# Overflow blocks of a mixture of experts: two places for their inputs and sums, products of neighbouring blocks interleaved, and the row gathers moved by one block

## The chip, the core and the metric

The kernel runs on 1 core of one Trainium2 chip. The metric is device time in microseconds (us) of one execution. The engines are TensorE (PE), VectorE (DVE), ScalarE (ACT), GpSimd (POOL) and SyncE (SP, which here only issues transfers). Each engine works through its own list of instructions in order, and they meet through semaphores.

## The reference, cut to what matters

A layer with a convolution, a sparse attention and a mixture of 64 experts (8 per token, 512 tokens, width 1024, hidden width 256) is followed by two more layers. The change lies in the mixture of experts:

```
D_MODEL = 1024
SEQ = 512
N_EXPERTS = 64
TOP_K_EXPERTS = 8
EXPERT_DIM = 256
DISPATCH_BLOCK = 128
...
def swiglu(x, w1, w3, w2):
    return (jax.nn.silu(x @ w1) * (x @ w3)) @ w2
...
    def expert_block(args):
        e, toks, gs = args
        xb = t[toks]
        return swiglu(xb, w1[e], w3[e], w2[e]) * gs[:, None]

    out = lax.map(expert_block, (block_e, row_tok.reshape(n_blk, DISPATCH_BLOCK),
                                 row_g.reshape(n_blk, DISPATCH_BLOCK)))
    routed = jax.ops.segment_sum(out.reshape(rows, D), row_tok, num_segments=n_tok)
```

## The kernel before, in words

**Experts.** A step n = 0 to 63 computes one expert for up to 128 of its tokens. POOL gathers their rows from `h2rows` into XG (an indirect transfer). PE turns them (`pe_xt`), ACT and DVE make a high and a low part (XTh, XTl), and PE forms three products for each pair of parts, six matmuls per chunk of weights ("a product" below is such a group of six). Four chunks give gate and up (PS bank 0 or 1), then come Silu on ACT (SG), the gated hidden row HG on DVE, two small transposes on PE, HHh on ACT and HHl on DVE, and two chunks of the down product into PS banks 6 and 7. ACT copies those to YS, and POOL adds YS to `expert_sum` in memory with an indirect transfer (the scatter, L2127). The weights come in through `eraw`; ACT splits off a high part (wh) and DVE the rest (wl) in a ring of four places.

**Overflow blocks.** Where an expert has more than 128 tokens, the rest is computed after the 64 experts in blocks of at most 128 rows. A table TB, made on the chip, holds their count at TB[2] and for block p its expert and a code for its row list. Each engine reads the count and enters block p by a branch (`more_blocks`, L2359). With these inputs there are 3 blocks (p = 0, 1, 2). The code is written per engine in `block_(p, i)`; i is 0 here. The gathers of blocks 0 and 1 are issued in steps 60 and 61, on POOL, by `more_gather` (L2140).

In block p POOL does, in this order: `more_gate(p + 1)` (copies the gate column of block p + 1, then `drain`), the copy YIXC of block p's list, `more_gather(p + 2)` (copies the list IDXC, `drain`, issues the gather), waits for YS, scatters (L2433), waits for the gather p + 2 and for its own scatter, and only then goes on with block p + 1. It gathers for blocks 3 and 4 as well, though there are none: PE turns the rows of block p + 1 in block p always, and the counts of the semaphores rest on it. After the last block POOL raises `rows_whole`, on which SP waits to load the sums from memory (YF, L2396), and PE for what follows.

PE does in block p: four up products, the transposes of block p + 1's rows (L2163), the transposes of HG (L2457), two down products. Inputs, sums and gated rows of the blocks have one place each (XTh[:, 0], PS[:, 0], HG[:, 0]). DVE and ACT split the weights of block p + 1's first two chunks behind block p's HHl and XTh.

## Time and profile before

| | |
|---|---|
| median of 3 runs | 2372.37 us (2371.32 to 2376.65) |
| the profiled execution's own time | 2377.54 us |
| its span | 2375.7 us |
| PE busy in the span | 2256.5 us (95%) |
| POOL busy in the span | 286.1 us (12%) |
| the overflow blocks, from their first product on PE to `rows_whole` | 1060.9 to 1108.0 us |

The span is the part of the execution that the profiler sees from the first to the last instruction; all places in the trace below are us from its start. The page says "PE 77%" for the chain that ended last, so most of the program is bound by PE; the stretch from 1052 to 1108 us is read apart, since the change touches nothing else.

### The profile page before, as it was taken

Reading aid. Unit: us, or ns where it says so; the run is one execution under the profiler, and the core shown is the slowest. Engines: PE = TensorE matmul, PEld = TensorE weight load, DVE = VectorE, ACT = ScalarE, POOL = GpSimd, SP = SyncE. Lnnn points to the kernel's source line nnn. Section 1 sums busy time; section 2 is a strip of 40 time slices with the busy share of each in tenths; the row PEclk is TensorE's granted clock in tenths of the full one; section 3 lists DMA queues with packets and bytes.
Section 4 is the critical chain, followed back from the end, with each engine's and each line's share of the span. In section 5 each row is a group of like instructions: output and inputs, shape, how many; then the busy total and the mean of one; then the engine's idle time right before and its main releaser. Section 6 shows DMA issues by size and latency. Waiting matters only on the chain.

```text
span 2375.7 us, 30540 instructions
## 1 busy us (share of the span) xinstructions
PE 2256.5 (95%) x10226; PEld 1760.5 (74%) x10226; DVE 1536.6 (65%) x2363; ACT 1198.8 (50%) x1774; POOL 286.1 (12%) x248
## 2 busy tenths in 40 slices
PE   7999999899999999985999999999999789999997
PEld 5776666778888888874766788888788557888885
DVE  7788766899999999985564643333452766433344
ACT  4432444588888888874334332333222763323333
POOL 0000000344334433431000000000020000000000
PEclk9998999999999999998999999999999999999999
DMA  8511245799999999995210132223222001322332
GB/s 330 176 59 58 80 169 172 266 354 397 388 393 387 391 392 393 391 334 156 80 63 18 62 107 96 97 97 107 89 98 98 19 27 61 116 98 92 102 106 80
DMA packets 107615, 415.70 MB, mean 175 GB/s; under 512 B 20305, under 2 KB 32849, under 8 KB 82784
## 3 DMA queue, kind: packets, MB, share of 16 engines
q1 hardware_dynamic: 87408, 378.47, 42.5%
q0 software_dynamic: 19648, 34.73, 5.9%
q8 instruction: 71, 1.16, 0.2%
q10 hardware_dynamic: 432, 0.87, 0.1%
q14 instruction: 56, 0.46, 0.1%
HBM read 409.23 MB, written 43.65 MB: 191 GB/s over the span
## 4 chain that ended last, share of the span: by engine, by line
PE 77%; DVE 9%; issue 5%; ACT 4%; DMA 2%; DVEq 2%; POOLq 0%; SPq 0%; POOL 0%; ACTq 0%
PE PS L298 22%; PE PS L300 21%; PE PS L299 21%; PE PS L714 3%; DVE wl L197 2%; PE PS L2007 2%; ACT wh L192 2%; PE PS L736 2%; PE PS L725 1%; DMA ada_wa<-wada 1%; DMA expert_sum<-YS,YIXC 1%; PE PS L2032 1%; DVE XTl L2060 1%; PE PS L1245 1%; DVEq L1285 1%
## 5 line engine op out<-in xcount | busy, mean ns | idle before, releaser
L197 DVE TENSOR_TENSOR wl<-raw,wh 128x1024 fp32r<-128x1024 f32 x239 | 292.5, 1225 | 357.2 <-ACT wh L192 351.0
L298 PE MATMUL PS<-HTh,wh 128*128 128x512 f32 x1248 | 499.9, 401 | 6.0 <-ACT V L881 2.2
L299 PE MATMUL PS<-HTl,wh 128*128 128x512 f32 x1248 | 487.8, 391 | 0.0
L300 PE MATMUL PS<-HTh,wl 128*128 128x512 f32 x1248 | 487.6, 391 | 0.0
L197 DVE TENSOR_TENSOR wl<-eraw,wh 128x1024 fp32r<-128x1024 f32 x384 | 457.7, 1219 | 16.6 <-ACT wh L192 13.6
L192 ACT ACTIVATE wh<-raw 128x1024 fp32r<-128x1024 f32 x239 | 252.0, 1056 | 369.9 <-PE PS L300 346.1
L192 ACT ACTIVATE wh<-eraw 128x1024 fp32r<-128x1024 f32 x384 | 392.6, 1054 | 17.0 <-PE PS L300 14.7
L298 PEld LDWEIGHTS PS<-HTh,wh 128*128 128x128 f32 x1248 | 235.3, 189 | 72.2 <-issue 13.6
L299 PEld LDWEIGHTS PS<-HTl,wh 128*128 128x128 f32 x1248 | 235.5, 189 | 50.2 <-issue 3.4
L300 PEld LDWEIGHTS PS<-HTh,wl 128*128 128x128 f32 x1248 | 235.3, 189 | 49.8
L298 PE MATMUL PS<-wh,XTh 128*128 128x512 f32 x536 | 221.1, 412 | 4.0 <-DVE wl L2192 2.8
L300 PE MATMUL PS<-wh,XTl 128*128 128x512 f32 x536 | 210.4, 392 | 0.0
L299 PE MATMUL PS<-wl,XTh 128*128 128x512 f32 x536 | 209.3, 390 | 0.0
L2127 POOL DMA_INDIRECT expert_sum<-YS,IDX x64 | 115.0, 1796 | 343.2 <-ACT YS L2091 211.3
L298 PE MATMUL PS<-AFh,wh 128*128 128x512 f32 x352 | 138.5, 394 | 0.0
L300 PE MATMUL PS<-AFh,wl 128*128 128x512 f32 x352 | 137.0, 389 | 0.0
L299 PE MATMUL PS<-AFl,wh 128*128 128x512 f32 x352 | 137.0, 389 | 0.0
L947 ACT ACTIVATE AFh<-AFf 128x512 f32 (+1 forms) x44 | 27.8, 632 | 182.4 <-DVEq L957 182.4
L298 PEld LDWEIGHTS PS<-wh,XTh 128*128 128x128 f32 x536 | 100.8, 188 | 23.4 <-DVE wl L2192 4.0
L300 PEld LDWEIGHTS PS<-wh,XTl 128*128 128x128 f32 x536 | 100.6, 188 | 22.2
L299 PEld LDWEIGHTS PS<-wl,XTh 128*128 128x128 f32 x536 | 101.2, 189 | 16.9
L298 PE MATMUL PS<-wh,HHh 128*128 128x512 f32 x268 | 105.6, 394 | 4.5 <-DVE HHl L2509 2.8
(412 smaller groups left out, 3439.7 us busy)
## 6 DMA issues: line engine op xcount, KB each, us to landing
eraw<-wstream SPq DMA_DIRECT2D x192, 1024.0 KB, 9.9
raw<-wstream SPq DMA_DIRECT2D x240, 512.0 KB, 3.3
ada_w<-wada SPq DMA_DIRECT2D x20, 512.0 KB, 5.9
eraw<-wexp SPq DMA_DIRECT2D x9, 1024.0 KB, 6.6
ada_wb<-wada SPq DMA_DIRECT2D x2, 2048.0 KB, 15.5
ada_l<-wada SPq DMA_DIRECT2D x8, 512.0 KB, 3.4
ada_g<-wada SPq DMA_DIRECT2D x2, 2048.0 KB, 10.3
expert_sum<-LM SPq DMA_DIRECT2D x8, 512.0 KB, 6.4
```

Source lines behind the costliest of these rows:

```text
L192: nc.scalar.activation(wh[:, ci % RING, :], src, ACT.Copy).then_inc(split_high, 1)
L197: nc.vector.tensor_tensor(wl[:, ci % RING, :], src, wh[:, ci % RING, :].bitcast(F32), ALU.subtract).then_inc(split_done, 1)
L298: nc.tensor.matmul(o, lh, rh, start=start, stop=False)
L299: nc.tensor.matmul(o, lh, rl, start=False, stop=False)
L300: return nc.tensor.matmul(o, ll, rh, start=False, stop=stop)
L714: mm = nc.tensor.matmul(PS[:, sbank(u, m), 0:P * (j + 1)], q[:, j * P:(j + 1) * P], k[:, 0:P * (j + 1)], start=x == 0, stop=x == len(prods ...
L725: mm = nc.tensor.transpose(PS[:, 4 + u % 2, kb * P:(kb + 1) * P], E_[:, u % 3, 0, kb * P:(kb + 1) * P], const("ident"))
L736: mm = nc.tensor.matmul(o, values(h, kb), Pt[:, u % 2, kb * P:(kb + 1) * P], start=kb == 0, stop=kb == j)
L947: nc.scalar.activation(ah(n, i), a_[:, n % 2, :], ACT.Copy).then_inc(s_h, 1)
L1245: nc.tensor.matmul(PS[:, 5 + n % 3, 0:P * (j + 1)], QI[b:b + HD, t, j * P:(j + 1) * P], KI[b:b + HD, 0:P * (j + 1)], start=True, stop=True ...
L2007: mm = nc.tensor.transpose(PS[:, 2 + m // 4, (m % 4) * P:(m % 4) * P + P], XG[:, n % 4, m * P:(m + 1) * P], const("ident"))
L2127: pool.indirect_dma_start(out=ysum[s], out_offset=bass.IndirectOffsetOnAxis(ap=IDX[:, 4 * n:4 * n + 1], axis=0), in_=YS[:, s, :], in_offse ...
```

## The change

**Places.** XTh, XTl, PS bank 0 or 1, SG, HG, HHh and HHl are used alternately by p % 2. **Order on PE, ACT and DVE.** Block 0's first two products move into step 63, in front of its down products, and for each later block the first two products (c = 0, 1) move into the block before, the second of them behind the transposes of HG. The transposes of block p + 1's rows move from the middle of block p to its front. ACT copies the sum of block p - 1 (YS) in block p, behind XTh; for the last block it does so at the end. **Order on POOL.** In step 63 POOL copies block 0's gate and gathers block 2, in front of the scatter of expert 63. In a block it scatters first and does `more_gate(p + 2)` and `more_gather(p + 3)` behind the scatter; in the last block it also waits for that last gather. **Branches.** `after` and `no_more` ask whether a further block comes; each is a branch of its own on its engine.

```
@@ -2164,33 +2164,73 @@
...
             def more_xh(act, p, i=0):
 
                 act.wait_ge(ov["xt"], i * GROUP + (p + 2))
-                if isinstance(i, int) and p == 0:
-                    act.wait_ge(chunk_used, up_end(E - 2))
-                nc.scalar.activation(XTh[:, 0, :], PS[:, 2:4, :].rearrange("p a b -> p (a b)"), ACT.Copy).then_inc(ov["xc"], 1)
+                if isinstance(i, int) and p < 2:
+                    act.wait_ge(chunk_used, up_end(E - 2 + p))
+                else:
+                    act.wait_ge(ov["used"], i * (6 * GROUP) + (6 * (p - 2) + 4 + ER))
+                nc.scalar.activation(XTh[:, p % 2, :], PS[:, 2:4, :].rearrange("p a b -> p (a b)"), ACT.Copy).then_inc(ov["xc"], 1)
 
...
             def more_high(act, p, c, i=0):
 
                 g = 6 * p + c
                 act.wait_ge(expert_arrived[g % ER // 2], i * (96 * GROUP // ER) + (96 * E // ER + 16 * (g // ER + 1)))
-                act.wait_ge(ov["used"], i * (6 * GROUP) + (g + ER - RING + 1))
-                act.wait_ge(chunk_used, EXPERT1 + RING if g > 2 else EXPERT1 + g + 1)
-                nc.scalar.activation(wh[:, g % RING, :], eraw[:, ER_PLACE[g % ER], :], ACT.Copy).then_inc(ov["high"], 1)
+                if isinstance(i, int) and p == 0 and c < 4:
+                    act.wait_ge(chunk_used, EXPERT1 + c + 1)
+                else:
+                    act.wait_ge(ov["used"], more_turn(p, c, i) + (ER - RING + 1))
+                nc.scalar.activation(wh[:, more_slot(p, c, i), :], eraw[:, ER_PLACE[g % ER], :], ACT.Copy).then_inc(ov["high"], 1)
...
+            def more_product(pe, p, c, i=0):
+
+                pe.wait_ge(ov["split"], more_turn(p, c, i) + 1)
+                for kk in range(2):
+                    w = slice(kk * 512, kk * 512 + 512)
+                    at = more_slot(p, c, i)
+                    wgh, wgl = wh[:, at, w], wl[:, at, w]
+                    if c < 4:
+                        r = slice((2 * c + kk) * P, (2 * c + kk) * P + P)
+                        mm = three_pass(PS[:, p % 2, :], XTh[:, p % 2, r], XTl[:, p % 2, r], wgh, wgl, c + kk == 0, c + kk == 4)
+                    else:
+                        r = slice((c - 4) * P, (c - 3) * P)
+                        mm = three_pass(PS[:, 6 + kk, :], HHh[:, p % 2, r], HHl[:, p % 2, r], wgh, wgl, c == 4, c == 5)
+                mm.then_inc(ov["used"], 1)
+
+            def after(eng, p, i):
+
+                return more[eng.engine] > i * GROUP + (p + 1)
+
+            def no_more(eng, p, i):
+
+                return more[eng.engine] <= i * GROUP + (p + 1)
...
@@ -2220,6 +2260,11 @@
                     if n + 1 < E:
                         pe_up(pe, n + 1, i, 0)
                     pe_ht(pe, n, i)
+                    if n + 1 == E:
+                        with pe.If(more[pe.engine] > 0):
+                            pe.wait_ge(ov["xl"], 1)
+                            more_product(pe, 0, 0)
+                            more_product(pe, 0, 1)
...
@@ -2256,6 +2301,10 @@
                     if n + 1 < E:
                         c0 = up_chunk(n + 1, 0)
                         split(c0 + 0 + AHEAD, at)
+                    if n + 1 == E:
+                        with act.If(more[act.engine] > 0):
+                            more_high(act, 0, 0)
+                            more_high(act, 0, 1)
...
                     if n + 1 == E:
                         with act.If(more[act.engine] > 0):
-                            for c in range(2):
-                                more_high(act, 0, c)
+                            more_high(act, 0, 2)
+                            more_high(act, 0, 3)
                     act_y(act, n, i)
...
@@ -2353,6 +2406,13 @@
                             pool.wait_ge(sem("places"), 4)
                         p = n + 4 - E
                         more_gather(pool, p, pool.value_load(TB[0:1, 3 * p + 1:3 * p + 2], min_val=0, max_val=255))
+                    elif n + 1 == E:
+                        pool.wait_ge(ov["rows"], 32)
+                        pool.sem_inc(passed_pool, 1)
+                        e0 = pool.value_load(TB[0:1, 0:1], min_val=0, max_val=E - 1)
+                        pool.tensor_copy(GS[:, 4:5], XG[:, 0, bass.ds(e0 + D, 1)]).then_inc(ov["gate"], 1)
+                        pool.drain()
+                        more_gather(pool, 2, pool.value_load(TB[0:1, 7:8], min_val=0, max_val=255))
                     scatter(pool, n, i)
...
@@ -2384,7 +2444,7 @@
                     for c in range(0, 6, 2):
                         g = 6 * p + c
                         at = ER_PLACE[g % ER]
-                        sp.wait_ge(ov["used"], i * (6 * GROUP) + (g + 2))
+                        sp.wait_ge(ov["used"], i * (6 * GROUP) + (g + (4 if c == 4 else 2)))
...
@@ -2425,9 +2485,8 @@
 
                 def block_(p, i):
                     y = 2 + p % 2
-                    more_gate(p + 1, i)
                     pool.tensor_copy(YIXC[:, y:y + 1], IDX[:, bass.ds(code_of(p, i), 1)])
-                    more_gather(pool, p + 2, code_of(p + 2, i), i)
+                    pool.drain()
                     pool.wait_ge(ov["y"], i * GROUP + (p + 2))
                     pool.sem_inc(passed_pool, 1)
                     pool.indirect_dma_start(out=ysum[0], out_offset=bass.IndirectOffsetOnAxis(ap=YIXC[:, y:y + 1], axis=0),
@@ -2435,10 +2494,15 @@
                                             compute_op=ALU.add).then_inc(ov["out"], 16)
                     pool.wait_ge(ov["rows"], i * (16 * GROUP) + 16 * (p + 3))
                     pool.sem_inc(passed_pool, 1)
+                    more_gate(p + 2, i)
+                    more_gather(pool, p + 3, code_of(p + 3, i), i)
+                    with pool.If(no_more(pool, p, i)):
+                        pool.wait_ge(ov["rows"], i * (16 * GROUP) + 16 * (p + 4))
+                        pool.sem_inc(passed_pool, 1)
                     pool.wait_ge(ov["out"], i * (16 * GROUP) + 16 * (p + 1))
                     pool.sem_inc(ov["sent"], 1)
-                pool.wait_ge(ov["rows"], 32)
-                more_gate(0, 0)
+                pool.wait_ge(ov["rows"], 48)
+                more_gate(1, 0)
                 more_blocks(pool, block_, lambda: pool.sem_inc(passed_pool, 1))
...
@@ -2447,51 +2511,56 @@
             @stage("pe")
             def _(pe):
                 def block_(p, i):
-                    pe.wait_ge(ov["xl"], i * GROUP + (p + 1))
-                    for c in range(6):
...
-                            pe.wait_ge(ov["y"], i * GROUP + (p + 1))
-                        pe.wait_ge(ov["split"], i * (6 * GROUP) + (g + 1))
...
+                    more_xt(pe, p + 1, i)
+                    more_product(pe, p, 2, i)
+                    more_product(pe, p, 3, i)
+                    with pe.If(after(pe, p, i)):
+                        pe.wait_ge(ov["xl"], i * GROUP + (p + 2))
+                        more_product(pe, p + 1, 0, i)
+                    pe.wait_ge(ov["hid"], i * GROUP + (p + 1))
+                    with pe.If(no_more(pe, p, i)):
+                        pe.sem_inc(ov["used"], 2)
+                    for f in range(2):
+                        mm = nc.tensor.transpose(PS[:, 4, f * P:(f + 1) * P], HG[:, p % 2, f * P:(f + 1) * P], const("ident"))
+                    mm.then_inc(ov["ht"], 1)
+                    with pe.If(after(pe, p, i)):
+                        more_product(pe, p + 1, 1, i)
+                    pe.wait_ge(ov["hl"], i * GROUP + (p + 1))
+                    pe.wait_ge(y_ready, E)
+                    pe.wait_ge(ov["y"], i * GROUP + (p + 1))
+                    more_product(pe, p, 4, i)
+                    more_product(pe, p, 5, i)
...
             @stage("act")
             def _(act):
                 def block_(p, i):
-                    for c in range(2, 6):
-                        more_high(act, p, c, i)
+                    more_xh(act, p + 1, i)
+                    if p or not isinstance(i, int):
+                        previous_y(p, i)
+                    with act.If(after(act, p, i)):
+                        more_high(act, p + 1, 0, i)
+                        more_high(act, p + 1, 1, i)
                     act.wait_ge(ov["used"], i * (6 * GROUP) + (6 * p + 4 + ER))
-                    nc.scalar.activation(SG[:, 0, :], PS[:, 0, 0:256], ACT.Silu).then_inc(ov["silu"], 1)
+                    nc.scalar.activation(SG[:, p % 2, :], PS[:, p % 2, 0:256], ACT.Silu).then_inc(ov["silu"], 1)
+                    with act.If(no_more(act, p, i)):
+                        act.sem_inc(ov["high"], 2)
+                    more_high(act, p, 4, i)
                     act.wait_ge(ov["ht"], i * GROUP + (p + 1))
-                    nc.scalar.activation(HHh[:, 0, :], PS[:, 4, 0:256], ACT.Copy).then_inc(ov["hc"], 1)
-                    more_xh(act, p + 1, i)
-                    with act.If(more[act.engine] > i * GROUP + (p + 1)):
-                        for c in range(2):
-                            more_high(act, p + 1, c, i)
-                    act.wait_ge(ov["used"], i * (6 * GROUP) + (6 * p + 6 + ER))
+                    nc.scalar.activation(HHh[:, p % 2, :], PS[:, 4, 0:256], ACT.Copy).then_inc(ov["hc"], 1)
+                    more_high(act, p, 5, i)
+                    with act.If(after(act, p, i)):
+                        more_high(act, p + 1, 2, i)
+                        more_high(act, p + 1, 3, i)
+                    with act.If(no_more(act, p, i)):
+                        previous_y(p + 1, i)
+
+                def previous_y(q, i):
+                    act.wait_ge(ov["used"], i * (6 * GROUP) + (6 * q + 2 + ER))
                     for s in range(2):
                         act.wait_ge(y_out[s], 16 * E // 2)
-                    act.wait_ge(ov["sent"], i * GROUP + (p + 1))
-                    nc.scalar.activation(YS[:, p % 2, :], PS[:, 6:8, :].rearrange("p a b -> p (a b)"), ACT.Copy).then_inc(ov["y"], 1)
+                    act.wait_ge(ov["sent"], i * GROUP + q)
+                    nc.scalar.activation(YS[:, (q + 1) % 2, :], PS[:, 6:8, :].rearrange("p a b -> p (a b)"), ACT.Copy).then_inc(ov["y"], 1)
                 more_blocks(act, block_, lambda: act.sem_inc(passed_act, 1))
...
                 def block_(p, i):
-                    for c in range(2, 6):
-                        more_low(dve, p, c, i)
+                    more_xl(dve, p + 1, i)
+                    with dve.If(after(dve, p, i)):
+                        more_low(dve, p + 1, 0, i)
+                        more_low(dve, p + 1, 1, i)
```

POOL, from the end of step 62 to the entry of the overflow blocks (XG are gathered rows, GS the gate columns, IDXC a list of rows, TB the table; `expert_sum<-YS` are the scatters; y_out0 and y_out1 say that scatters have landed). Before:

```order
L2100 COPY GS<-XG 128x1 [waits xg_in3,hid_full]
L2127 DMA expert_sum<-YS,IDX 512x1024 [waits y_out0,y_ready]
L2127 DMA expert_sum<-YS,IDX 512x1024 [waits y_out1,y_ready]
L2414 TENSOR_LOAD TB [waits more_rows]
L2414 ISA x2
L2423 ISA
L2423 COPY GS<-XG 128x1
```

Now:

```order
L2100 COPY GS<-XG 128x1 [waits xg_in3,hid_full]
L2127 DMA expert_sum<-YS,IDX 512x1024 [waits y_out0,y_ready]
L2412 TENSOR_LOAD TB [waits more_rows]
L2412 ISA x2
L2413 ISA
L2413 COPY GS<-XG 128x1
L2415 TENSOR_LOAD TB
L2415 ISA x2
L2146 ISA [waits more_rows]
L2146 COPY IDXC<-IDX 128x1
L2153 DMA XG<-h2rows,IDXC 128x1088 [waits more_xt]
L2127 DMA expert_sum<-YS,IDX 512x1024 [waits y_out1,y_ready]
```

Between the scatters of experts 62 and 63 stand now a gate copy, a list copy and the gather of block 2, with two drains that this list does not show.

POOL, a block that is neither the first nor the last. Before, from behind its gate copy to its scatter:

```order
L2423 COPY GS<-XG 128x1
L2409 TENSOR_LOAD TB
L2409 ISA x2
L2429 ISA
L2429 COPY YIXC<-IDX 128x1
L2409 TENSOR_LOAD TB
L2409 ISA x2
L2146 ISA [waits more_rows]
L2146 COPY IDXC<-IDX 128x1
L2153 DMA XG<-h2rows,IDXC 128x1088 [waits more_xt]
L2433 DMA expert_sum<-YS,YIXC 512x1024 [waits more_y]
```

Now, from its list copy to the branch behind its gather:

```order
L2488 COPY YIXC<-IDX 128x1
L2492 DMA expert_sum<-YS,YIXC 512x1024 [waits more_y]
L2474 TENSOR_LOAD TB [waits more_rows,more_hid]
L2474 ISA x2
L2483 ISA
L2483 COPY GS<-XG 128x1
L2469 TENSOR_LOAD TB
L2469 ISA x2
L2146 ISA [waits more_rows]
L2146 COPY IDXC<-IDX 128x1
L2153 DMA XG<-h2rows,IDXC 128x1088 [waits more_xt]
L2499 COMPARE_AND_BRANCH
```

The scatter (L2433, now L2492) stood behind the gather and stands now ahead of it, with the gate copy between them.

PE, the place where block p + 1's rows are turned (L2163 reads XG; HG are gated rows, wh and wl weights). Before, in the middle of block 2:

```order
L299 MATMUL PS<-wl,XTh 128x512
L300 MATMUL PS<-wh,XTl 128x512
L2163 MATMUL PS<-K,XG 128x128 [waits more_rows]
L2163 MATMUL PS<-K,XG 128x128 x7
L2457 MATMUL PS<-K,HG 128x128 [waits more_hid]
L2457 MATMUL PS<-K,HG 128x128
L298 MATMUL PS<-wh,HHh 128x512 [waits more_y,more_split,y_ready,more_hl]
```

Now, at the entry of block 2:

```order
L300 MATMUL PS<-wh,HHl 128x512
L2424 COMPARE_AND_BRANCH
L2163 MATMUL PS<-K,XG 128x128 [waits more_rows]
L2163 MATMUL PS<-K,XG 128x128 x7
L298 MATMUL PS<-wh,XTh 128x512 [waits more_split]
L299 MATMUL PS<-wl,XTh 128x512
L300 MATMUL PS<-wh,XTl 128x512
L298 MATMUL PS<-wh,XTh 128x512
```

The transposes and their wait for `more_rows` stand now ahead of the block's products, where before its four up products came first.

## Rows read from the trace of the kernel before

**Rows 1.** Windows, core 0: busy us (instructions) per engine, clock, DMA share, GB/s.

```profile
1098.10:1108.10 10.00, 0.00 (x0) 0.00 (x0) 3.70 (x6) 3.97 (x4) 2.66 (x2) 0.67 0.24 33
```

**Rows 2.** Chain that ended last, in order of time: start us, us, what.

```profile
1099.97 5.05 DMA expert_sum<-YS,YIXC
1105.19 2.82 issue
```

**Rows 3.** Drains on POOL and scatters ahead, one window each: ns min/median/max, start us.

```profile
L2147 POOLq DRAIN  x1: 11498/11498/11498, 1026.5 to 1026.5; - x1
...
L2127 POOL DMA_INDIRECT expert_sum<-YS,IDX x1: 1601/1601/1601, 1025.0 to 1025.0; - x1
DMA to landing us min/median/max: 8.6/8.6/8.6
...
L2147 POOLq DRAIN  x1: 9370/9370/9370, 1040.3 to 1040.3; - x1
...
L2127 POOL DMA_INDIRECT expert_sum<-YS,IDX x1: 2518/2518/2518, 1040.9 to 1040.9; - x1
DMA to landing us min/median/max: 8.7/8.7/8.7
...
L2424 POOLq DRAIN  x1: 4877/4877/4877, 1065.1 to 1065.1; - x1
...
L2127 POOL DMA_INDIRECT expert_sum<-YS,IDX x1: 1557/1557/1557, 1064.3 to 1064.3; - x1
DMA to landing us min/median/max: 5.5/5.5/5.5
...
L2147 POOLq DRAIN  x1: 243/243/243, 1097.3 to 1097.3; - x1
```

**Rows 4.** Timeline of POOL: start us, us, instruction, [idle before it].

```profile
1054.65 1.58 POOL L2127 DMA_INDIRECT expert_sum<-YS,IDX  x1 [0.17 <-issue]
...
1088.52 2.58 POOL L2433 DMA_INDIRECT expert_sum<-YS,YIXC  x1 [0.31 <-issue]
...
1097.34 0.18 POOL L2146 COPY IDXC<-IDX 128x1 int32 x1 [0.57 <-issue]
...
1098.48 1.07 POOL L2153 DMA_INDIRECT XG<-h2rows,IDXC  x1 [0.96 <-issue]
```

**Rows 5.** Timeline of PE, rows of the stretch from 1060 to 1100.

```profile
1060.87 0.40 PE L298 MATMUL PS<-wh,XTh 128*128 128x512 f32 x1
...
1063.37 0.39 PE L300 MATMUL PS<-wh,XTl 128*128 128x512 f32 x1
...
1089.69 0.50 PE L298 MATMUL PS<-wh,XTh 128*128 128x512 f32 x1 [0.42 <-DVE wl L2192]
...
1092.55 1.04 PE L2163 MATMUL PS<-K,XG 128*128 128x128 f32 x8
```

**Rows 6.** Timeline of ACT, and one row of DVE, 1060 to 1100.

```profile
1062.41 1.03 ACT L2091 ACTIVATE YS<-PS 128x1024 f32<-128x1024 f32 x1 [4.61 <-DMA expert_sum<-YS,IDX]
...
1075.03 3.89 ACT L2186 ACTIVATE wh<-eraw 128x1024 fp32r<-128x1024 f32 x4
...
1098.10 1.02 ACT L2494 ACTIVATE YS<-PS 128x1024 f32<-128x1024 f32 x1 [2.62 <-PE PS L300]
...
1076.11 4.63 DVE L2192 TENSOR_TENSOR wl<-eraw,wh 128x1024 fp32r<-128x1024 f32 x4 [1.13 <-ACT wh L2186]
```

**Rows 7.** Landing: five gathers L2153, the one at 1098.5, three scatters L2433.

```profile
DMA to landing us min/median/max: 2.5/4.3/7.4
...
DMA to landing us min/median/max: 3.1/3.1/3.1
...
DMA to landing us min/median/max: 5.1/6.0/6.3
```

**Rows 8.** A loop's branch back on SP, window 1134 to 1135.

```profile
L2399 SPq COMPARE_BRANCH  x1: 53/53/53, 1134.7 to 1134.7; - x1
L2399 SPq FUSED_REGOPS  x1: 50/50/50, 1134.8 to 1134.8; - x1
```

63 lines of the change are left out of this document (28 added, 35 removed).

## The prediction

> **What bounds the kernel now.** I first read the page: PE is busy for 95% of the span, but not in the stretch of the overflow blocks. The windows then show what ends that stretch: from 1098.1 to 1108.1 PE executes nothing [rows 1]. The chain of waits names who is waited for: the scatter of block 2, 5.05 us from 1099.97, and then 2.82 us in which POOL gets from its last block to `rows_whole` [rows 2]. So what the blocks cost is set by when POOL raises `rows_whole`, at 1108.0 us, and PE's last down product counts only through the scatter behind it. A change that shortens PE's blocks is worth what it takes off POOL's last transfer, and what it adds behind that transfer counts in full. The next views are therefore POOL's own: its drains, its timeline and the landings.
>
> **What a drain on POOL waits for.** The drain that began at 1065.1 took 4.88 us and ended at 1069.98; the scatter issued just before it, at 1064.3, landed 5.5 us later, at 1069.8. The one at 1040.3 took 9.37 us, to 1049.7; the scatter of 1040.9 landed after 8.7 us, at 1049.6. The one at 1026.5 took 11.5 us, to 1038.0, though the scatter of 1025.0 had landed at 1033.6. The drain at 1097.3, with every transfer of POOL landed, took 0.24 us [rows 3]. I read this so: a drain behind an indirect transfer that is still under way holds POOL until it has landed, to 0.2 us in two cases, longer in one. Before, the blocks escape this: each block waits for its scatter and its gather anyway before it drains, and gather and scatter go out close together (1098.48 [rows 4] and 1099.97).
>
> **The change, part by part.**
>
> *Step 63 on PE.* The first two products of block 0 go in front of the down products of expert 63. The same 24 matmuls follow each other in another order. One matmul starts every 0.227 us (11 steps from 1060.87 to 1063.37 [rows 5]), so a product of six takes 1.37 us. The new first one waits for the DVE half of its weights, which comes about when the first down product started before, since DVE and ACT run through the same steps. Both orders end near 1063.7 (1063.37 + 0.39): worth nothing. ACT gets something: the high parts for c = 2 and 3 are now made ahead of YS, which waited 4.6 us for a landing at 1062.4 [rows 6], so products (0,2) and (0,3) no longer wait for them.
>
> *Step 63 on POOL.* Behind the scatter of expert 62 (issued at 1054.65 [rows 4]) come gate copy, drain, list copy, drain and gather 2. The drain waits for that scatter. The nearest landings are 8.7 and 5.5 us [rows 3], so it ends between 1060 and 1065; I take 1065.2, as the stretch is as full of weight loads as it was for the 8.7. From a drain's end to the next gather's start I count 1.8 us: about 0.66 for the table load and the next copy (IDXC came 0.57 behind a copy of 0.18) and 1.14 from IDXC to the gather at 1098.48 [rows 4]. Gather 2 starts at 1067.0, the scatter of expert 63 at 1068.4 instead of 1064.3, and it lands at 1074 to 1077. Only YS of block 0 asks for it, at 1077.4, so this costs at most 1 us.
>
> *Blocks 0 and 1 on PE.* Block 0: about 1 us of transposes (1.04 with the end of the last [rows 5]), two products (2.73), to 1067.7 with small starts. Then (1,0) waits for its weights: ACT makes YS, XTh and one high part (each 0.92 to 1.0 us; four high parts take 3.89), DVE XTl and one rest (four take 4.63, so 1.14 each [rows 6]), to 1069.2. This wait of 1.5 us stands where the Silu to HHl chain stood, which is now covered. Then (1,0), HG's transposes, (1,1), (0,4), (0,5), with 0.3 and small starts, to 1075.5. Block 1 in the same way to 1087.1. PE is then some 2 us ahead of before.
>
> *POOL in the blocks.* YS of block 0 now stands in ACT's list behind XTh of block 2: it ends at 1078.5, and with the 0.8 us that a scatter takes to start, scatter 0 is at 1079.3 (1099.97 [rows 2] is 0.85 behind the end of its YS, 1098.10 + 1.02 [rows 6]). A scatter of a block lands after 5.1 to 6.3 us; I take 5.8, the mean of the three. A gather of a block lands after 2.5 to 7.4; the last one took 3.1 [rows 7]. Gathers 3 to 5 run as that one and the 2.5 do, with no weight loads beside them: I take 2.8. So the drain of `more_gate` lets go at 1085.3, gather 3 starts at 1087.1 and lands at 1089.9. PE has wanted it since 1087.1, since the transposes now stand at the block's front. From there: transposes, XTh and YS of block 1 (1.14 + 1.03 + 0.95 and small steps) to 1093.0, scatter 1 at 1093.8 (before 1088.5 [rows 4]), landed 1099.6, gather 4 at 1101.6 (0.2 + 1.8), landed 1104.4. The new drain ahead of the next scatter waits for that, and 0.95 us later, at 1105.4, scatter 2 starts. PE's part isn't late for it: block 2 from its third product took 8.4 us (1089.69 [rows 5] to 1098.1 [rows 6]); with 1.1 of transposes in front and about 1.2 for a weight part that DVE now makes inside the chain it ends at about 1100, YS at 1101. Even 2 us more for a lower clock after PE's idle time stays hidden under the 4.5 us that are left.
>
> *The tail.* Scatter 2 at 1105.4, landing 5.8, drain 0.2, 1.8 to gather 5, its landing 2.8, which the new wait for the last block asks for, 0.1, and the 2.82 of [rows 2]: `rows_whole` at 1119.0 instead of 1108.1.
>
> *Branches.* In blocks 0 and 1 each `no_more` is passed over: one on PE, DVE and POOL, two on ACT. The nearest row is the loop of SP, whose branch back at 1134.7 is followed by its target at 1134.8 [rows 8]. I take 0.1 us each, inside other waits. The other end is the 2.82 us of the far branch [rows 2]. The Trainium skill ("Runtime: NRT & Kernel Launch", Instruction fetch mechanics) says that a taken branch whose target lies outside the code window must fetch it first, and this speaks against the change: by it a short branch could cost what the far one does where it falls on the window's edge.
>
> **The sum.** Scatter 2 is later by 5.4 us (1105.4 against 1099.97). Behind it 13.6 us (5.8 + 2.0 + 2.8 + 3.0) stand in place of 8.1 (1108.1 - 1100.0): 5.5 more. Together +10.9 us. The profiled execution took 2377.54 us, so 2388.4 for such a one; the median of the runs shown is 2372.37, 5.2 below it, and the forecast for a median is 2383.3 us, 0.46% slower. What follows `rows_whole` is the same and moves as a whole.
>
> Bounds: with 5.1 and 2.5 us for the landings +7.9; with 6.3 and 4.3 us, and the scatter of expert 63 landing after 9 to 10 us, +18. That is 2380 to 2390.5 for the forecast's own case.
>
> **The rivals.**
>
> *The drain does not wait for transfers* (the 11.5 us case doesn't fit its scatter, so the two fits could be chance; the two agree to 0.2 us, which speaks against). Then gather 3 starts at 1083.5, PE never waits for rows, and PE ends at 1096.8, scatter 2 is at 1098.7, 1.3 us earlier. But gather 5 goes out about 4.2 us behind scatter 2 and lands 7.0 behind it, 1.9 later than a scatter's 5.05. Sum +0.6: 2373.0 us, no change.
>
> *The blocks become bound by PE alone* (the other side). If weights are ready in time and gathers and scatters pass each other freely, PE has after 1063.7 sixteen products (21.9 us), three sets of transposes and HG (about 3.5) and the last chain from Silu to HHl (2.9, what is left of the 8.4 us above behind four products): 1092.0 instead of 1098.1, so `rows_whole` 6.1 us earlier, 2366.3 us. It decides from the point where POOL's round from scatter to scatter is under PE's 11 us; it is 5.8 + 2.0 + 2.8 + 0.95 = 11.6 at my values, before any wait for PE, and the tail's extra 5.5 must vanish as well. So it is unlikely.
>
> *Short branches fetch code.* POOL passes `no_more` twice; at 2.9 us each this adds 5.8, to +16.7: 2389.1 us. It is the rule of the skill named above, carried to every short branch; the SP row speaks against it.
>
> **How the numbers follow.** Forecast 0.70, no wait in the drain 0.15, short branches 0.08, PE alone 0.07. About 0.2% (4.7 us) is what a measurement of this kernel can tell from no change. Slower by more: 0.70 + 0.08 = 0.78; within: 0.15; faster: 0.07. The forecast's own range holds too little by itself, so the range takes in the no-change case: 2373 to 2391 us.
>
> **What would show it.** Right: two drains of 5 to 6 us per block on POOL (behind each scatter), scatter 1 at least 13 us behind scatter 0, PE waiting 2 to 4 us for XG at the front of block 2, gather 5 on the chain that ended last, `rows_whole` near 1119. Wrong: drains under 1 us behind a scatter that is under way; then the no-change case holds. Wrong in size only: landings outside 5 to 6.3 and 2.5 to 4.3 us, since three scatters and three gathers stand in a row and each us of either counts three times.

## The result, and the profile after

| | kernel before | changed kernel |
|---|---|---|
| median of 8 runs each, us | 2376.14 | 2385.96 |
| ratio, 95% interval | | 1.0045 (1.0036 to 1.0054) |
| profiled execution, us | 2377.54 | 2390.31 |
| mean granted clock | 0.983 | 0.978 |

The change makes the kernel 0.45% slower by the ratio, some 10.7 us (the two medians differ by 9.8); the forecast was +10.9 us. The forecast time of 2383.3 us lies 2.7 below the measured one, mostly because it was added to a median of 3 runs, 2372.37, where 8 runs give 2376.14. Two single profiles are compared from fixed marks. The **stretch** runs from the two HG transposes of expert 63 on PE (L2032) to PE's first instruction behind `rows_whole` (L471): 1055.05 to 1108.11 = 53.1 us before, 63.6 us now, so 10.6 us more. The spans differ by 12.8 us; the other 2.2 us lie elsewhere (3.5 less ahead of the stretch, 5.7 more behind it) and belong to these two executions. The timeline of PE in the changed kernel:

```profile
1051.52 0.44 PE L2032 MATMUL PS<-K,HG 128*128 128x128 f32 x2 [2.74 <-DVE HG L2072]
...
1065.60 0.47 PE L298 MATMUL PS<-wh,XTh 128*128 128x512 f32 x1 [1.40 <-DVE wl L2209]
...
1087.11 1.88 PE L2163 MATMUL PS<-K,XG 128*128 128x128 f32 x8 [3.21 <-DMA XG<-h2rows,IDXC]
...
1115.16 1.22 PE L471 MATMUL PS<-K 128*128 128x512 f32 x1 [16.55 <-POOLq L2509]
```

At 1087.11 PE waits 3.21 us for gathered rows at the front of block 2, and the eight transposes behind that wait take 1.88 us where eight took 1.04 [rows 5]. Before `rows_whole` it stands idle for 16.55 us, where ten were seen before [rows 1]. The chain that ended last, in the same columns as [rows 2]:

```profile
1084.34 2.72 DMA XG<-h2rows,IDXC
...
1110.10 2.19 DMA XG<-h2rows,IDXC
...
1112.54 2.53 issue
```

It now runs through two gathers. On POOL, the timeline with the gathers (L2153) and scatters (L2127 for experts, L2492 for blocks), which answers to [rows 4]:

```profile
1063.52 1.08 POOL L2153 DMA_INDIRECT XG<-h2rows,IDXC  x1 [0.99 <-issue]
1064.90 2.01 POOL L2127 DMA_INDIRECT expert_sum<-YS,IDX  x1 [0.31 <-issue]
...
1075.92 1.57 POOL L2492 DMA_INDIRECT expert_sum<-YS,YIXC  x1 [3.10 <-ACT YS L2563]
...
1084.34 1.07 POOL L2153 DMA_INDIRECT XG<-h2rows,IDXC  x1 [0.97 <-issue]
...
1091.83 1.60 POOL L2492 DMA_INDIRECT expert_sum<-YS,YIXC  x1 [6.21 <-ACT YS L2563]
...
1098.99 1.07 POOL L2153 DMA_INDIRECT XG<-h2rows,IDXC  x1 [0.97 <-issue]
...
1102.14 2.35 POOL L2492 DMA_INDIRECT expert_sum<-YS,YIXC  x1 [1.87 <-DMA XG<-h2rows,IDXC]
```

From scatter to the next gather POOL needs 8.42 us (1075.92 to 1084.34), 7.16 and 7.96. Most of what lies in between is a drain. One window each of the drain behind a block's scatter, and of that scatter with its landing, as in [rows 3]:

```profile
L2484 POOLq DRAIN  x1: 4787/4787/4787, 1076.6 to 1076.6; - x1
...
L2492 POOL DMA_INDIRECT expert_sum<-YS,YIXC x1: 1574/1574/1574, 1075.9 to 1075.9; - x1
...
DMA to landing us min/median/max: 5.4/5.4/5.4
...
L2484 POOLq DRAIN  x1: 4564/4564/4564, 1092.5 to 1092.5; - x1
...
L2492 POOL DMA_INDIRECT expert_sum<-YS,YIXC x1: 1605/1605/1605, 1091.8 to 1091.8; - x1
...
DMA to landing us min/median/max: 5.1/5.1/5.1
...
L2484 POOLq DRAIN  x1: 5342/5342/5342, 1102.8 to 1102.8; - x1
...
L2492 POOL DMA_INDIRECT expert_sum<-YS,YIXC x1: 2346/2346/2346, 1102.1 to 1102.1; - x1
...
DMA to landing us min/median/max: 5.9/5.9/5.9
```

The three drains behind the scatters end at 1081.4, 1097.1 and 1108.1. The scatters land at 1081.3 (1075.92 + 5.4), 1096.9 and 1108.0. The block's other drain, ahead of its scatter (L2489), waits for the gather in the same way: it took 1.99 us from 1085.2 and 1.49 from 1099.8, so it ended at 1087.2 and 1101.3, and the gathers landed at 1087.0 (1084.34 + 2.7) and 1101.2 (1098.99 + 2.2).

### The profile page after: what moved, and what is told of

Its sections match the earlier page's. It is cut to its first block, busy times and chain, and to the rows that moved or that the text cites. A ratio compares the mean times of both kernels' runs of the same rounds, so it can differ in the third digit from the quotient of the medians.

```text
span 2388.5 us, 30598 instructions
## 1 busy us (share of the span) xinstructions
PE 2263.4 (95%) x10226; PEld 1765.8 (74%) x10226; DVE 1536.5 (64%) x2363; ACT 1199.2 (50%) x1774; POOL 290.8 (12%) x251
## 4 chain that ended last, share of the span: by engine, by line
PE 76%; DVE 10%; issue 5%; ACT 4%; DVEq 2%; DMA 1%; POOLq 1%; POOL 0%; ACTq 0%; SPq 0%
PE PS L298 21%; PE PS L300 21%; PE PS L299 21%; DVE wl L197 3%; PE PS L714 2%; PE PS L2007 2%; PE PS L736 2%; ACT wh L192 2%; PE PS L725 1%; DVEq L1285 1%; DVE XTl L2060 1%; DVE M L1282 1%; PE PS L2032 1%; PE PS L1245 1%; DMA eraw<-wstream 1%
## 5 line engine op out<-in xcount | busy, mean ns | idle before, releaser
L192 ACT ACTIVATE wh<-eraw 128x1024 fp32r<-128x1024 f32 x384 | 392.7, 1054 | 17.6 <-PE PS L300 13.6
L299 PEld LDWEIGHTS PS<-HTl,wh 128*128 128x128 f32 x1248 | 235.5, 189 | 50.3 <-issue 3.9
L2127 POOL DMA_INDIRECT expert_sum<-YS,IDX x64 | 115.4, 1803 | 335.2 <-ACT YS L2091 202.6
L298 PEld LDWEIGHTS PS<-wh,XTh 128*128 128x128 f32 x536 | 101.6, 189 | 24.2 <-issue 6.2
## 6 DMA issues: line engine op xcount, KB each, us to landing
ada_g<-wada SPq DMA_DIRECT2D x2, 2048.0 KB, 10.3
```

The source lines that it names most:

```text
L192: nc.scalar.activation(wh[:, ci % RING, :], src, ACT.Copy).then_inc(split_high, 1)
L298: nc.tensor.matmul(o, lh, rh, start=start, stop=False)
L299: nc.tensor.matmul(o, lh, rl, start=False, stop=False)
L2127: pool.indirect_dma_start(out=ysum[s], out_offset=bass.IndirectOffsetOnAxis(ap=IDX[:, 4 * n:4 * n + 1], axis=0), in_=YS[:, s, :], in_offse ...
```

## The experiments

A second mark is needed where an edit acts ahead of the stretch. The **long stretch** begins at the HG transposes of expert 61, two pairs of L2032 earlier: 1033.54 to 1108.11 = 74.6 us before, 1029.98 to 1115.16 = 85.2 us changed.

**1. Lists and gate column ahead of the scatter.** In each block POOL makes its copies, with their drains, before it waits for the sums, and the gather follows right behind the scatter.

```
@@ changed kernel, block_ on POOL
-                    pool.drain()
+                    pool.wait_ge(ov["rows"], i * (16 * GROUP) + 16 * (p + 3))
+                    pool.sem_inc(passed_pool, 1)
+                    pool.tensor_copy(IDXC[:, b:b + 1], IDX[:, bass.ds(code_of(p + 3, i), 1)])
+                    more_gate(p + 2, i)
                     pool.wait_ge(ov["y"], i * GROUP + (p + 2))
...
-                    more_gate(p + 2, i)
-                    more_gather(pool, p + 3, code_of(p + 3, i), i)
```

> The changed kernel, but POOL copies the list and the gate column of the later block ahead of the scatter, with the one drain there, so that nothing drains between scatter and gather. The stretch is counted from the two HG transposes of expert 63 on PE to rows_whole: before 53.0 us, changed 63.6. Theory (a drain behind a scatter waits for its landing, and that is the whole loss): gather 3 goes out within 2 us of scatter 0, PE does not wait for rows in front of block 2, the last gather lands with the last scatter; stretch 51.5 to 53.5, so 10 to 12 us less than changed and 0 to 1.5 less than before. Rival (the loss comes from the new order on PE or from the short branches, which stay): stretch stays at 60 or more.

Measured: ratio 0.9993 (0.9979 to 1.0008), stretch 1048.98 to 1102.81 = 53.8 us. Timeline of POOL (scatter, gather behind it, block 0 and block 2), then of PE:

```profile
1073.38 1.57 POOL L2496 DMA_INDIRECT expert_sum<-YS,YIXC  x1 [2.46 <-ACT YS L2568]
1075.26 1.54 POOL L2501 DMA_INDIRECT XG<-h2rows,IDXC  x1 [0.30 <-issue]
...
1094.51 1.60 POOL L2496 DMA_INDIRECT expert_sum<-YS,YIXC  x1 [1.65 <-ACT YS L2568]
1096.42 1.51 POOL L2501 DMA_INDIRECT XG<-h2rows,IDXC  x1 [0.31 <-issue]
```

```profile
1048.98 0.44 PE L2032 MATMUL PS<-K,HG 128*128 128x128 f32 x2 [2.75 <-DVE HG L2072]
...
1081.19 1.03 PE L2163 MATMUL PS<-K,XG 128*128 128x128 f32 x8
...
1102.81 2.08 PE L471 MATMUL PS<-K 128*128 128x512 f32 x2 [10.22 <-POOLq L2514]
```

The gather now starts 1.9 us behind its scatter, PE doesn't wait for rows at block 2 (1081.19 has no idle time in front), and the last gather and the last scatter land together (1096.42 + 3.5 against 1094.51 + 5.2). Of the 10.6 us lost, 9.8 come back from the place of a few copies and drains alone; the stretch is 0.3 us above the upper edge that was expected.

**2. No gather for blocks that don't exist.**

```
@@ changed kernel, block_ on POOL
-                    more_gate(p + 2, i)
-                    more_gather(pool, p + 3, code_of(p + 3, i), i)
-                    with pool.If(no_more(pool, p, i)):
-                        pool.wait_ge(ov["rows"], i * (16 * GROUP) + 16 * (p + 4))
-                        pool.sem_inc(passed_pool, 1)
+                    with pool.If(after(pool, p, i)):
+                        more_gate(p + 2, i)
+                        more_gather(pool, p + 3, code_of(p + 3, i), i)
```

> The changed kernel, but the last block does no gate copy and no gather behind its scatter. Theory (in series behind the last scatter: drain to its landing, 2.0 us of lists, the gather's landing): only the part behind the landing goes, 4.2 to 5 us; stretch 58.6 to 59.4. Rival (the last gather lands beside the scatter anyway): less than 1 us, stretch about 63.

Measured: ratio 1.0025 (1.0014 to 1.0036), stretch 1054.28 to 1113.60 = 59.3 us, as expected. The tail behind scatter 2 is 7.8 us (1105.83 to 1113.60) and not 13.0, so the drain, the lists and the gather there are worth 5.2 us. The stretch falls by 4.3 only, since scatter 2 came 0.9 us later behind the mark: in this profile the 24 matmuls of step 63 took 8.4 us at a granted clock of 0.64, and 7.2 at 0.76 in the changed kernel's.

**3 and 4. One part alone.** First POOL's new order with PE, ACT and DVE as before; then their new order with POOL's order as before. The edit of the second (the first is the diff's POOL part on the kernel before):

```
@@ changed kernel, POOL back to the order of before
-                    elif n + 1 == E:
...
-                        more_gather(pool, 2, pool.value_load(TB[0:1, 7:8], min_val=0, max_val=255))
...
+                    more_gate(p + 1, i)
                     pool.tensor_copy(YIXC[:, y:y + 1], IDX[:, bass.ds(code_of(p, i), 1)])
-                    pool.drain()
+                    more_gather(pool, p + 2, code_of(p + 2, i), i)
```

> The kernel before with the changed POOL order alone (step 63 and blocks); PE, ACT and DVE as before. Theory: gather 3 is late by the drain but PE turns its rows in the middle of block 2, so only the tail (5.5 us) and up to 2 us of a later scatter of expert 63 are paid: stretch 58.5 to 60.5. Rival (the loss comes from the order on PE, ACT and DVE): stretch 53.

> The changed kernel with the POOL order of before (gathers two blocks ahead, ahead of the scatter, nothing added in step 63). Theory: rows are now wanted at a block's front, but gather p + 2 only goes out once scatter p - 1 has landed and the lists are copied, so PE waits 4 to 7 us for rows at the front of blocks 1 and 2; no gather in the tail; stretch 60 to 66. Rival (interleaving pays by itself and POOL's order is the whole loss): stretch 47 to 52.

Measured: POOL's part alone 1.0030 (1.0019 to 1.0041), stretch 1055.06 to 1113.45 = 58.4 us, a hair under its range; PE's part alone 1.0062 (1.0043 to 1.0080), stretch 1052.83 to 1120.95 = 68.1 us, 2 us above its range. In the latter PE waits for rows at the front of two blocks:

```profile
1077.62 1.97 PE L2163 MATMUL PS<-K,XG 128*128 128x128 f32 x8 [4.07 <-DMA XG<-h2rows,IDXC]
...
1095.44 1.97 PE L2163 MATMUL PS<-K,XG 128*128 128x128 f32 x8 [5.04 <-DMA XG<-h2rows,IDXC]
```

So POOL's part costs 5.3 us by itself, nearly all behind the last scatter (1100.76 to 1113.45 = 12.7 us where 8.1 stood), while PE still finds its rows. PE's part by itself costs 15.0, more than both together, since POOL's order of before asks for the rows later still. The two costs therefore don't add up. In the changed kernel the other 5.3 us appear only when PE asks for its rows at a block's front: one half of the loss is a longer tail, the other a late gather that meets an earlier wait.

**5 and 6. The drains taken away.** Where POOL reads its own small copy (the gate column, both index columns), the copy raises a semaphore and POOL waits for that. Both kernels also wait for block 0's rows ahead of block 1's gather.

```
-                pool.tensor_copy(IDXC[:, b:b + 1], IDX[:, bass.ds(code, 1)])
-                pool.drain()
+                pool.tensor_copy(IDXC[:, b:b + 1], IDX[:, bass.ds(code, 1)]).then_inc(sem("more_list"), 1)
+                pool.wait_ge(sem("more_list"), i * GROUP + (p + 1))
+                pool.sem_inc(passed_pool, 1)
```

> The changed kernel, with each drain of GpSimd behind a small copy (the gate column, the two index columns, step 63's too) replaced by a wait of GpSimd for the semaphore that the copy itself raises; ahead of the gather of block 1 it also waits for the rows of block 0. Order of copies, gathers and scatters as in the changed kernel. Stretch from the two HG transposes of expert 63 on TensorE to rows_whole: 53.0 us before, 63.6 us as changed. Theory (the drain waits until the transfers issued ahead of it have landed, and that is the whole loss): the gather of block 3 goes out 2 to 3 us behind scatter 0, TensorE has no idle time for rows at the front of block 2, tail behind scatter 2 about 8.3 us; stretch 52 to 54 us, time 2370 to 2377 us. Rival (it is the place of the gather behind the scatter on the queue that costs, not the drain): the landings grow to 8 us or more, stretch 60 us or more, time above 2381 us.

> The kernel before, with the same replacement of each drain and nothing else. Its last stage waits for the scatter's landing in any case, so theory: the stretch stays at 52 to 53.5 us, while the two gaps of 12.0 and 6.9 us on GpSimd ahead of the gathers of steps 60 and 61 close, the gate columns of the last experts come earlier, and TensorE loses its waits of 1.1 and 2.7 us for gated rows there: time 0 to 5 us below the kernel before, ratio 0.998 to 1.0. Rival (drains cost something in the overflow blocks of the kernel before as well): stretch 50 us or less.

Measured for the changed kernel: 1.0012 (1.0000 to 1.0023), stretch 1046.00 to 1105.56 = 59.6 us, long stretch from 1027.86 77.7 us. This misses the 52 to 54 expected, and its time is 3 us above the range. By the long stretch 7.5 us are back. Block 2 on POOL and the end of expert 63 on PE:

```profile
1095.25 1.60 POOL L2496 DMA_INDIRECT expert_sum<-YS,YIXC  x1 [2.93 <-ACT YS L2567]
1096.30 1.46 POOL L2485 COPY GS<-XG 128x1 f32 x1
...
1100.50 1.08 POOL L2154 DMA_INDIRECT XG<-h2rows,IDXC  x1 [0.99 <-POOL IDXC L2146]
```

```profile
1046.00 0.44 PE L2032 MATMUL PS<-K,HG 128*128 128x128 f32 x2 [0.69 <-DVE HG L2072]
1048.72 0.77 PE L298 MATMUL PS<-wh,XTh 128*128 128x512 f32 x1 [2.28 <-DVE wl L2210]
```

Two things were left out of the expectation. Without a drain the gather still goes out 5.25 us behind the scatter, not 2 to 3: the gate copy there lasts 1.46 us where it took 0.18 elsewhere, and table load, list copy and the step to the gather follow. So PE still waits 0.81 us for rows at the front of block 2, and the tail is 10.3 us (1095.25 to 1105.56), not 8.3. And of the 3.4 us that the drains of the expert steps gave back (from the HG transposes of expert 61 to those of 63: 18.1 us, 21.5 before), only 0.7 are left at block 0's transposes: PE now waits 2.28 us for block 0's weights where it waited 0.79, and the 24 matmuls behind took 8.3 us at a granted clock of 0.64, not 7.2 at 0.76. From block 0's transposes to `rows_whole` it takes 48.5 us (1057.06 to 1105.56) where the changed kernel took 55.3: 6.8 us is what the drains among the blocks cost it. The rival (the place of the gather on the queue) does no better: its gathers landed after 3.6 and 2.2 us, not 8.

For the kernel before, the same edit gives 0.9980 (0.9968 to 0.9991), long stretch 71.5 us, 3.0 less, as expected: PE's wait at expert 63's transposes is 0.69 us where it was 2.74, and the one of 1.14 us a step earlier is gone.

```profile
1027.78 0.38 PE L2032 MATMUL PS<-K,HG 128*128 128x128 f32 x2
...
1037.10 0.38 PE L2032 MATMUL PS<-K,HG 128*128 128x128 f32 x2
...
1045.91 0.44 PE L2032 MATMUL PS<-K,HG 128*128 128x128 f32 x2 [0.69 <-DVE HG L2072]
...
1099.32 1.22 PE L471 MATMUL PS<-K 128*128 128x512 f32 x1 [11.45 <-POOLq L2449]
```

The drains did cost something in the kernel before, but in its last expert steps and not, as the prediction read rightly, in its blocks (the stretch stays at 53.4 us). Without any drains the order of before is still 6.2 us ahead of the changed one (71.5 against 77.7): the drains are the largest part of the loss and not all of it.

**7. Four edits together.** No drains, no last gather, `rows_whole` raised inside the last block, and ACT and DVE making the next block's first weight chunk ahead of its transposed rows.

```
@@ changed kernel without drains, ACT
-                    more_xh(act, p + 1, i)
-                    if p or not isinstance(i, int):
-                        previous_y(p, i)
                     with act.If(after(act, p, i)):
                         more_high(act, p + 1, 0, i)
+                    more_xh(act, p + 1, i)
+                    with act.If(after(act, p, i)):
                         more_high(act, p + 1, 1, i)
+                    if p or not isinstance(i, int):
+                        previous_y(p, i)
```

> As the run without drains, and besides: the gather and gate column for blocks that don't exist left out of the last block, rows_whole raised inside the last block ahead of the branch that ends it, and ScalarE and VectorE making the first weight chunk of the next block ahead of its transposed rows, with the copy of the sums behind that. Theory: 2.5 us less for the branch, 0 to 0.5 for the last gather, 1 to 3 for TensorE's waits for weights: stretch 47 to 51 us, ratio to the kernel before 0.994 to 0.998. Rival (TensorE's order has no more to give, or the sums' copy comes later and takes it back): stretch 51.5 to 54 us, ratio 0.998 to 1.0.

Measured: 0.9989 (0.9976 to 1.0002), stretch 1048.79 to 1102.73 = 53.9 us, long stretch 72.1. That is in the rival's range, not in the expected one. The tail is 5.6 us (scatter 2 at 1097.13), so that part came. From the reordered weights little is left at the end: block 2's sums start to be copied 64.6 us behind the mark, against 65.2 in run 1 and 65.5 in run 5. PE's timeline shows why, from block 1's front to block 2's:

```profile
1070.85 1.03 PE L2164 MATMUL PS<-K,XG 128*128 128x128 f32 x8
...
1082.86 1.09 PE L2164 MATMUL PS<-K,XG 128*128 128x128 f32 x8 [2.03 <-DMA XG<-h2rows,IDXC]
```

Block 1 took 10.0 us of PE (1070.85 to 1080.83), where it took 11.9 in run 5: its wait for weights (1.58 us) is gone. But PE then waits 2.03 us for rows, since POOL's lists still stand behind the scatter here, and block 2's last 12 matmuls took 5.5 us at a granted clock of 0.50, against 4.6 at 0.63 in run 5. The new weight order with the lists ahead of the scatter wasn't run.

**8. A drain in the expert steps.**

```
@@ kernel before, POOL, step(n, i), behind scatter(pool, n, i)
+                    if 16 <= n < 56 and n % 4 == 0:
+                        pool.drain()
```

> The kernel before with one more drain of GpSimd behind the scatter in ten of the expert steps (16 to 52, every fourth), where nothing else is changed. Theory (a drain ends when the transfers issued ahead of it by GpSimd have landed): each of the ten drains lasts as long as its scatter takes to land, less up to 0.7 us, and goes up and down with it (correlation near 1), whatever the spread of the landings. Rival (a drain has a fixed length or waits only for the descriptors to be written): ten durations that agree with each other within 0.5 us while the landings spread.

Measured (one profile, 2398.8 us). The drains of this line as a group, ns min/median/max:

```profile
L2358 POOLq DRAIN  x10: 9221/9790/11196, 612.4 to 977.8; - x10
```

They last 9.2 to 11.2 us here, among the weight stream, against 4.6 to 5.3 behind a block's scatter, where little else is transferred. The trace of before gives landings of 8.4 to 11.5 us, median 9.3, for the expert steps' scatters (500 to 1012 us), and 5.1 to 6.3 for the blocks' [rows 7]. A fixed length is out. The pairing of each drain with its own scatter couldn't be read: this trace has no landing for single scatters of that line.

**9 to 11. A version that beats both, and what PE's order is worth.** The first is the kernel before without drains, with the last block's needless gather left out and `rows_whole` raised inside the last block. The second has in addition the changed kernel's order on POOL, mended as in run 1. The third has the changed kernel's order on PE, ACT and DVE as well.

```
@@ kernel before without drains, block_ on POOL
-                    more_gather(pool, p + 2, code_of(p + 2, i), i)
+                    with pool.If(after(pool, p, i)):
+                        more_gather(pool, p + 2, code_of(p + 2, i), i)
...
                     pool.sem_inc(ov["sent"], 1)
+                    with pool.If(no_more(pool, p, i)):
+                        whole()
...
+                def whole():
+                    for s in range(2):
+                        pool.wait_ge(y_out[s], 16 * E // 2)
+                    pool.sem_inc(sem("rows_whole"), 1)
```

> The kernel before without drains, and in the last block it gathers no further rows, so that its scatter isn't behind a gather, and raises rows_whole ahead of the branch that ends the block. Measured from the HG transposes of expert 61 on TensorE to rows_whole: 74.6 us before, 71.5 us without drains. In the run without drains the last sums stood ready at 1088.9 us and the scatter went out at 1091.3; the branch took 2.5 us. Theory: 1.5 to 2 us and 2.5 us less, 67 to 68 us, ratio to the kernel before 0.995 to 0.998. Rival (the landing of the last scatter grows, or something else ends last): 70 us or more.

> TensorE, ScalarE and VectorE in the order of the kernel before; GpSimd in the order of the changed kernel with its lists and gate columns ahead of the wait for the sums, the gather right behind the scatter, no drains, no gather for blocks that don't exist, rows_whole raised inside the last block. Theory (without the drains TensorE, at 11.7 us a block, is the bound of the stage whatever GpSimd's order): within 1 us of the kernel before mended in the same way, 67 to 68.5 us from the HG transposes of expert 61 to rows_whole. Rival (the two places for the sums let TensorE run ahead): 65 us or less.

> GpSimd's order mended as in the run with the order of before on TensorE (no drains, lists and gates early, rows_whole inside the last block), but with the changed kernel's interleaved order on TensorE, ScalarE and VectorE. Theory (the interleaved order itself gains nothing here: its first block ends 6 us later, since block 1's first two products stand ahead of block 0's last, its later blocks take 10.6 us instead of 11.7, and three blocks don't win that back): 70 to 72.5 us from the HG transposes of expert 61 to rows_whole, 2 to 5 us more than with the order of before on TensorE. Rival (only GpSimd held the interleaved order back): 67 us or less, not slower than the order of before.

| | ratio to before (95%) | long stretch, us |
|---|---|---|
| before's order everywhere, mended | 0.9943 (0.9928 to 0.9959) | 65.3 |
| changed order on POOL, mended | 0.9947 (0.9930 to 0.9964) | 66.7 |
| changed order everywhere, mended | 0.9978 (0.9964 to 0.9992) | 71.9 |

The first kernel's timeline of PE (the mark, the first matmul of product (0,2), and the one behind `rows_whole`), and the end of its chain:

```profile
1030.57 0.38 PE L2032 MATMUL PS<-K,HG 128*128 128x128 f32 x2
...
1056.42 0.50 PE L298 MATMUL PS<-wh,XTh 128*128 128x512 f32 x1 [0.60 <-DVE wl L2193]
...
1095.84 4.63 PE L471 MATMUL PS<-K 128*128 128x512 f32 x5 [7.48 <-POOLq L2439]
```

```profile
1088.39 1.03 ACT YS L2514
...
1090.27 5.28 DMA expert_sum<-YS,YIXC
```

From scatter 2 to `rows_whole` it takes 5.6 us instead of 8.1. It is 13.6 us (0.57% of 2378.5) faster than the kernel before; its long stretch explains 9.3 of them in the one profile taken; where the other 4.3 lie wasn't looked for. The stretch is 1.7 us better than expected, and the second run differs from it by 1.4 us, not under 1. Both come in the main from one place, the matmuls of step 63 behind its wait for HHl. Windows of PE there, first and second kernel: stretch, us, busy us (instructions), granted clock, DMA share, GB/s:

```profile
1050.10:1055.40 5.30, 5.30 (x23) 1.00 1.04 400
```

```profile
1052.20:1059.10 6.90, 6.88 (x23) 0.75 1.02 367
```

The third, with PE's interleaved order and nothing left on POOL that holds it, PE's timeline (product (0,2) at 1058.63; transposes L2164 at a block's front, so the block before ends there):

```profile
1028.16 0.38 PE L2032 MATMUL PS<-K,HG 128*128 128x128 f32 x2
...
1049.02 0.77 PE L298 MATMUL PS<-wh,XTh 128*128 128x512 f32 x1 [2.29 <-DVE wl L2210]
...
1058.63 0.50 PE L298 MATMUL PS<-wh,XTh 128*128 128x512 f32 x1 [0.22 <-DVE wl L2210]
...
1063.05 0.47 PE L298 MATMUL PS<-wh,XTh 128*128 128x512 f32 x1 [1.38 <-DVE wl L2210]
...
1069.52 1.03 PE L2164 MATMUL PS<-K,XG 128*128 128x128 f32 x8
...
1074.88 0.47 PE L298 MATMUL PS<-wh,XTh 128*128 128x512 f32 x1 [1.58 <-DVE wl L2210]
...
1081.19 1.03 PE L2164 MATMUL PS<-K,XG 128*128 128x128 f32 x8
...
1100.02 1.22 PE L471 MATMUL PS<-K 128*128 128x512 f32 x1 [7.49 <-POOLq L2492]
```

Behind the mark its blocks end on PE after 41.4, 53.0 and 64.4 us (the last is where the copy of its sums starts, 1092.56); in the first kernel of the table the copies, released by PE, start after 34.3, 46.0 and 57.8. A block takes 11.7 and 11.4 us against 11.8 and 11.8. I had expected 10.6: that was the distance of the copies of the sums, which ACT makes behind other work, and not that of the blocks on PE. The interleaved order doesn't shorten a block in this version. It covers the chain from Silu to HHl (0.93 us idle, and 0.41 for weights) and waits 1.38 and 1.58 us for weights instead, and in the last block, with nothing to cover it, the chain stands open again (1.21 and 1.39 us idle). What it costs comes ahead: product (0,2) starts 30.5 us behind the mark against 25.9, with 2.29 us of wait for weights in step 63 and transposes in front; and block 0 carries two more products (2.5 us more to its end). A good part of the difference is the clock. The 24 matmuls of step 63 took 8.5 us here at a granted clock of 0.65, against 5.7 at 1.00 in the first kernel and 7.4 at 0.77 in the second; block 2's last 12 took 4.6 at 0.63, against 3.1 at 1.00 in both. Of the 5.1 us between the second and the third kernel 2.7 are such slower matmuls. Whether the interleaved order brings the lower clock about, by where it lets PE wait, isn't shown.

## Why the prediction was right, point by point

**What bounds the kernel**: right. What ends the stretch is when POOL raises `rows_whole`; run 2 changed only POOL's work behind the last scatter, and the tail fell by 5.2 us and the stretch by 4.3.

**The drain waits for the landing**: right. Five drains fit the landing ahead of them to 0.2 us (two before, three after), and so do five more in runs 2 and 3 (4.5 to 4.8 us long). Run 8 shows their length following the traffic, and run 5 shows 6.8 us among the blocks leaving with them. The rest of what POOL lost is the time of the copies themselves where they stand behind a scatter: run 1 moves both and gets 9.8 back. The misfit that the prediction named stays open: the drain of 1026.5 outlasted its scatter's landing by 4.4 us [rows 3], and its twin in the changed kernel took 11.8 us.

Of the signs that the prediction set, one came in another form: not two drains of 5 to 6 us in each block, but one of 4.6 to 5.3 behind the scatter and a shorter one ahead of the next, which waits for the gather (2.0 and 1.5 us).

**Step 63**: the places right, with some luck. Counted from the HG transposes, gather 2 was put at 12.0 us and came at 12.0 (1063.52); the scatter of expert 63 at 13.4, and came at 13.4. But the drain ahead of them ended after 8.9 us, not 10.2, and the way from there to gather 2 took 3.1 us, not 1.8, since the copy of the list and the drain behind it took 1.2 to 1.3 us each: two misses of 1.3 us that cancel. Scatter 0 was put at 24.2, and came at 24.4. PE's wait for (1,0) was put at 1.5 us and was 1.40.

**POOL in the blocks**: the mechanism right, two terms off in opposite ways. Scatter 1 was put 14.5 us behind scatter 0 and came 15.9 behind: scatter to gather took 8.42 us and not 7.8, and PE's eight transposes behind the wait took 1.88 us and not 1.14. Scatter 2 was put 11.6 us behind scatter 1 and came 10.3 behind, since that scatter landed after 5.1 us and gather 4 after 2.2, not 5.8 and 2.8. Together scatter 2 stood at 50.6 us behind the mark, forecast 50.3. The agreement to 0.3 us is therefore better than the terms deserve.

**The tail**: 13.0 us (1102.14 to 1115.16), forecast 13.6; the gather landed after 2.19 us instead of 2.8.

**Branches**: right for POOL. The three `no_more` of POOL took 44 to 58 ns each, while from the last gather's landing over the far branch to `rows_whole` it took 2.53 us (chain above), which runs 7 and 9 to 11 save by raising `rows_whole` ahead of that branch (5.4 to 5.6 us from scatter 2 to `rows_whole`, not 8.1). The rival of short branches that fetch code is out.

```profile
L2499 POOLq COMPARE_BRANCH  x3: 44/50/58, 1084.1 to 1109.9; - x3
```

**PE in blocks 0 and 1**: right. In the changed kernel block 1 ended on PE 32.4 us behind the mark (its next wait, for rows, began at 1083.9). In run 1, where PE doesn't wait for rows, it ended 32.2 us behind the mark (1081.19 - 1048.98), forecast 32.1 (1087.1 - 1055.05), with two products of block 2 done: some 2 us ahead of before. They are lost in the last block, as the forecast had it too (its end at 45, measured 43.6, before 43.1).

**The rivals**: "no wait in the drain" is out by the pairs of drains and landings. "Bound by PE alone, -6.1 us" is out too: with POOL's part mended the interleaved kernel is level with before (run 1), since its waits for weights and the open chain of the last block take what this rival counted as gained. What no rival named is the opposite: with the drains gone and the lists ahead, the order of before on PE is the faster one, by 5.1 us in the long stretch of one profile each, 2.7 of it clock (their ratios differ by 0.31%, some 7 us).

## What to carry to other kernels

- Before an instruction is moved behind a transfer that its own engine issues, look at what orders the engine against itself. A drain that costs 0.2 us with nothing under way costs a whole landing behind a scatter. Make the small tables ahead of the wait for the data, and let transfers follow each other directly; where only one's own small copy is meant, wait for that copy's semaphore.
- If the last thing before a join is a transfer, everything put behind it counts in full, needless prefetches and the branch out of the loop as well: 5.2 and 2.5 us here.
- Interleaving covers an idle chain only as far as the covering work has its own inputs. Here it put a wait for weights in the chain's place (run 7 could move that wait away in block 1, and then the rows came late), delayed the first block, and left the last one's chain open. To judge such an order, measure it in a kernel in which its engine is the bound.

## What the runs showed that was not expected

- A copy of 128 elements on POOL takes 0.18 us alone and 0.75 to 1.5 us right behind the issue of a scatter (1.50 at 1076.93 behind scatter 0, 0.75 at 1092.89 behind scatter 1, 1.46 at 1096.30 in run 5). With the table loads and the list copy behind it, it is 5.2 us from scatter to gather without any drain.
- The same matmuls (23 starts in each window) at the same place in step 63 took 5.3 us at a granted clock of 1.00 (2.4 GHz) in one kernel and 6.9 at 0.75 in the other (a part of them at 1.2 GHz). What PE did just before hardly differs (idle for 0.72 and 0.93 us, against 0.69 and 0.93), so the cause stays open. It is worth 1.6 us here, as much as some of the edits above, so a single profile can't rank them.
- The kernel before had more to give than the change aimed at: edits on POOL alone make it 13.6 us faster. 9.3 of them lie in the long stretch of the profile, 1.6 of these being the clock; the second kernel, with the lower clock, has 7.9 there.
